# One Trainium2 core, two transformer blocks: the order and place of the small transfers at the front, column sums of the modulation, gates of the experts' rows, and two norms behind the experts

## What is computed

```python
# block 1
mod = silu(c) @ w_mod + b_mod                 # 6 x 1024 columns, for c and for c_ctx
h, hc = modulate(rmsnorm(x)), modulate(rmsnorm(ctx))
q, k, v, r = split(h @ w_in)                  # the same for hc
z = (h @ w_ga) @ w_gb + b_g                   # rank 16, two directions
logdecay = log_sigmoid(z) / 16
o = gated linear attention, forwards and backwards over the tokens
x = x + g1 * ((rmsnorm(o) * silu(r)) @ w_out)
h2 = modulate(rmsnorm(x))
scores = sigmoid(h2 @ w_router)               # 16 experts, 2 chosen per token, in one group of 4
f = sum over chosen experts of gate * ((silu(h2 @ w1) * (h2 @ w3)) @ w2)
x = rmsnorm(x + g2 * f) * final_g
# block 2: x and ctx_2 are normed and modulated with mod_w_2, then latent and grouped attention
# (ab), a second residual, window attention and a short convolution (cd), a third residual
```

## Time and profile before

| | us |
|---|---|
| median of 3 runs | 1193.26 |
| the runs | 1191.73, 1193.26, 1199.64 |
| the profiled execution, whole | 1190.98 |
| its span, first to last instruction | 1189.2 |
| PE busy | 1020.5 (86%) |
| PE weight loads busy | 551.7 (46%) |
| DVE busy | 366.7 (31%) |
| ACT busy | 297.6 (25%) |
| mean granted PE clock | 0.943 |
| HBM read | 211.26 MB |

### The profile page before, as it was taken

How to read it: one execution, slowest core, us unless ns; L and a number is a source line. 1 busy time by engine, 2 the same in 40 slices (tenths; PEclk the granted TensorE clock), 3 DMA queues, 4 the chain that set the end, 5 groups by cost and what they waited for, 6 DMA issues and landing times.

```text
span 1189.2 us, 12358 instructions
## 1 busy us (share of the span) xinstructions
PE 1020.5 (86%) x4434; PEld 551.7 (46%) x4435; DVE 366.7 (31%) x850; ACT 297.6 (25%) x674; POOL 23.0 (2%) x41
## 2 busy tenths in 40 slices
PE   0899979989977877878768899989999897897998
PEld 0454436546543322323222555557555443575773
DVE  0200273561424100000000413057676511254451
ACT  0410422322223000000000232146665501214330
POOL 2000000000000000000000100000000000000000
PEclk9899899998977989889898999989999999898999
DMA  9925031779055699998999520201645212142220
GB/s 272 365 77 208 0 142 36 280 265 372 2 202 222 235 396 396 398 350 303 397 397 394 190 71 13 87 33 35 230 161 142 72 35 71 43 146 96 71 71 36
DMA packets 102233, 217.43 MB, mean 183 GB/s; under 512 B 5909, under 2 KB 8137, under 8 KB 102057
## 3 DMA queue, kind: packets, MB, share of 16 engines
q1 hardware_dynamic: 94480, 206.45, 47.9%
q10 hardware_dynamic: 6312, 6.03, 1.6%
q0 software_dynamic: 1392, 4.31, 1.4%
HBM read 211.26 MB, written 5.51 MB: 182 GB/s over the span
## 4 chain that ended last, share of the span: by engine, by line
PE 69%; DMA 13%; DVE 7%; ACT 5%; issue 3%; ACTq 2%; POOLq 0%; SPq 0%; POOL 0%; DVEq 0%
PE bank L527 24%; DMA arena<-in_w_up_e_dram 10%; PE bank L539 8%; PE bank L725 8%; PE bank L796 4%; PE bank L495 3%; PE bank L879 3%; PE bank L898 3%; PE bank L889 3%; DMA arena<-in_mod_w_dram 2%; PE bank L482 1%; PE bank L713 1%; PE bank L738 1%; PE bank L577 1%; PE bank L791 1%
## 5 line engine op out<-in xcount | busy, mean ns | idle before, releaser
L527 PE MATMUL bank<-arena 128*128 128x512 f32 (+3 forms) x768 | 308.3, 560 | 6.6 <-ACT arena L1128 5.1
L527 PEld LDWEIGHTS bank<-arena 128*128 128x128 f32 x768 | 145.7, 192 | 159.5 <-issue 143.1
L725 PE MATMUL bank<-arena 128*64 128x512 f32 x544 | 139.8, 671 | 32.3 <-issue 29.6
L725 PEld LDWEIGHTS bank<-arena 128*64 128x64 f32 x544 | 52.4, 153 | 118.8 <-issue 113.5
L539 PE MATMUL bank<-arena 128*128 128x256 f32 (+1 forms) x384 | 99.3, 418 | 2.8 <-ACT arena L1449 1.5
L539 PEld LDWEIGHTS bank<-arena 128*128 128x128 f32 x384 | 72.7, 191 | 31.7 <-issue 22.2
L738 PE MATMUL bank<-arena 128*64 128x512 f32 x272 | 62.1, 597 | 9.6 <-ACT arena L1298 9.0
L495 PE MATMUL bank<-arena,silu_c 128*32 128x512 f32 x384 | 51.2, 657 | 19.5 <-ACT silu_c L1141 10.1
L1296 ACT ACTIVATE arena<-bank 128x256 f32<-128x256 f32 x16 | 6.1, 383 | 217.3 <-PE bank L725 217.3
L1857 DVE TENSOR_TENSOR arena<-arena,bank 128x256 f32<-128x256 f32 x16 | 6.7, 422 | 154.5 <-ACT arena L1296 154.5
L879 PE MATMUL bank<-arena 64*128 64x512 f32 (+3 forms) x160 | 49.3, 561 | 4.5 <-ACT arena L1535 2.3
(11 more groups left out here) (303 smaller groups left out, 1014.7 us busy)
## 6 DMA issues: line engine op xcount, KB each, us to landing
arena<-in_w_gate_e_dram SPq DMA_DIRECT2D x16, 2048.0 KB, 16.9
arena<-in_w_up_e_dram SPq DMA_DIRECT2D x16, 2048.0 KB, 21.9
arena<-in_w_down_e_dram SPq DMA_DIRECT2D x16, 2048.0 KB, 20.2
arena<-in_w_mod_dram SPq DMA_DIRECT2D x12, 2048.0 KB, 9.5
arena<-in_mod_w_dram SPq DMA_DIRECT2D x12, 2048.0 KB, 10.9
arena<-in_gla_w_in_dram SPq DMA_DIRECT2D x6, 2048.0 KB, 12.8
arena<-in_cd_w_in_dram SPq DMA_DIRECT2D x6, 2048.0 KB, 7.8
arena<-in_ab_w_in_dram SPq DMA_DIRECT2D x5, 2048.0 KB, 9.1
```

What stands on the lines that cost most here:

```text
L527: mm = pe.matmul(ps[:, 0:n], lhs[:, k, tile * P:(tile + 1) * P], w[:, k, c0:c0 + n], start=(k == 0), stop=(k == kd_ - 1))
L725: mm = pe.matmul(up_b[64 * j:64 * j + 64, :], h[:, k, :], w13[:, :, k, 256 * j:256 * j + 256], start=(k == 0), stop=(k == KC - 1), tile_po ...
```

## The change

- **Small transfers.** `con` is reordered and split: the first 147 columns come through ACT among the rows, the rest through POOL. `gate_a`, `gate_b`, the rest of `con`, `w_route`, the gains and `final_row` are issued by POOL, the first of them after the bank `row3`, `w_route` after `z31`.
- **First fills.** SP's order is mod0, mod1, x, ctx, mod2, mod3, k; mod0 to mod3 lie in slots 0, 1, 3, 5, and the ring goes on with k in slot 2.
- **Column sums.** `mod_cols` transposes 4 x 128 columns; DVE adds the four quadrants with a reduction and then the bias.
- **Low, z, router, gate 1.** The two directions of `low` use two column strips, those of z two row strips (partitions 0 and 32), alternating. The router's product is made with `w_route` as weights in four column strips, copied to `parts` by ACT and DVE, and summed and turned with `sum_parts`. `gate(1)` becomes one bank with the two halves on partitions 0 to 63 and 64 to 127.
- **Experts.** DVE multiplies the rows with that gate as it evicts them.
- **Behind.** The gathers have a semaphore for each tile; DVE does three operations a tile; ACT sums the squares of x and of x * final_g together, and the second scale is worked out from both; ACT does `columns_0(2)` first.

```diff
         for m in range(4):
-            load_mod(m)
+            l, c = mod_chunks[m]
+            loads.append((f"mod{m}", [(slice(0, P), slice(0, KC), cols_of(a["w_mod"][0], 512 * c, 512))],
+                          (0, 1, 3, 5)[m], KC, 512))
...
+        early_columns = cols["ones"][0]
+        con_rest_in = sem("con_rest_in")
...
-                    mm = pe.matmul(ps[:, 2 * c:2 * c + 2], mod_rows[:, m % 2, c * P:(c + 1) * P], sum_quadrants,
-                                   start=True, stop=True)
+                    mm = pe.transpose(ps[:, c * P:(c + 1) * P], mod_rows[:, m % 2, c * P:(c + 1) * P], ident)
...
+                if u == 1:
+                    ps = banks.open(pe, "gate1_1", gate_bc, 4)
+                    for h in range(2):
+                        mm = pe.matmul(ps[64 * h:64 * h + 64, :], ones[:, 0:64], gate_diag[:, 4 * h:4 * h + 4, :],
+                                       start=True, stop=True, tile_position=(0, 64 * h))
+                    banks.filled("gate1_1", mm)
+                    return
...
-            for z in range(2):
-                ps = banks.open(pe, f"low{z}", low_ready, z + 1)
-                for k in range(KC):
-                    mm = pe.matmul(ps[0:GATE_RANK, :], gate_a[:, k, z, :], hT[:, k, :],
-                                   start=(k == 0), stop=(k == KC - 1))
-                banks.filled(f"low{z}", mm)
+            pe.wait_ge(small_w_in, 16 * 2)
+            ps = banks.open(pe, "low", low_ready, 2)
+            for k in range(KC):
+                for z in range(2):
+                    mm = pe.matmul(ps[32 * z:32 * z + GATE_RANK, :], gate_a[:, k, z, :], hT[:, k, :],
+                                   start=(k == 0), stop=(k == KC - 1), tile_position=(0, 32 * z))
+            banks.filled("low", mm)
...
+            for h in range(HG):
+                for z in range(2):
+                    r = slice(32 * z, 32 * z + GATE_RANK)
+                    ps = banks.open(pe, f"z{h}{z}", z_ready, 2 * h + z + 1)
+                    mm = pe.matmul(ps[:, :], gate_b[r, h * DK:(h + 1) * DK], low[r, :], start=True, stop=True,
+                                   tile_position=(32 * z, 0))
+                    banks.filled(f"z{h}{z}", mm)
...
+            pe.wait_ge(route_in, 16)
+            ps = banks.open(pe, "parts", parts_copied, 4)
+            for k in range(KC):
+                j = k % 4
+                mm = pe.matmul(ps[32 * j:32 * j + NE, 0:T], w_route[:, k, :], h2T[:, k, :],
+                               start=(k < 4), stop=(k >= 4), tile_position=(0, 32 * j))
+            banks.filled("parts", mm)
+            pe.wait_ge(parts_copied, 4)
             ps = banks.open(pe, "logits", logit_exp, 1)
             for t in range(TT):
-                for k in range(KC):
-                    mm = pe.matmul(ps[:, t * NE:(t + 1) * NE], h2T[:, k, t * P:(t + 1) * P], w_route[:, k, :],
-                                   start=(k == 0), stop=(k == KC - 1))
+                mm = pe.matmul(ps[:, t * NE:(t + 1) * NE], parts[:, t * P:(t + 1) * P], sum_parts, start=True, stop=True)
...
-            sp.dma_start(X[:, 0:2, :], a["x"][0].rearrange("(t p) d -> p t d", p=P)).then_inc(x_in, 16)
-            sp.dma_start(X[:, 2:4, :], a["ctx"][0].rearrange("(t p) d -> p t d", p=P)).then_inc(ctx_in, 16)
...
-            for ld in loads[:N_BEFORE]:
+            for i, ld in enumerate(loads[:N_BEFORE]):
+                if i == 2:
+                    sp.dma_start(X[:, 0:2, :], a["x"][0].rearrange("(t p) d -> p t d", p=P)).then_inc(x_in, 16)
+                    sp.dma_start(X[:, 2:4, :], a["ctx"][0].rearrange("(t p) d -> p t d", p=P)).then_inc(ctx_in, 16)
...
-            act.dma_start(con[:, :], a["constants"]).then_inc(con_in, 16)
-            for n, r, half in row_list:
+            for i, (n, r, half) in enumerate(row_list):
+                if i == 4:
+                    act.dma_start(con[:, 0:early_columns], a["constants"][:, 0:early_columns]).then_inc(con_in, 16)
...
+                    act.activation(gate_rows[:, 1, 0:512], ps[:, :], ACT.Copy).then_inc(gate_bc, 2)
...
-                act.wait_ge(z_ready, 4 * z + 4)
+                act.wait_ge(z_ready, 7 + z)
...
-            act.wait_ge(x_moe, 2)
-            norm(3, y_tok[:, :, 0, :], lambda t: None)
             columns_0(2)
-            act.wait_ge(block1_done, 2)
-            norm(4, view(HIGH, 4, D), lambda t: None)
+            for t in range(TT):
+                act.wait_ge(x_moe, t + 1)
+                act.activation(y_tok[:, t, 1, :], X[:, t, :], ACT.Square, accum_out=sums[:, t:t + 1])
+                act.wait_ge(xf_ready, t + 1)
+                ins = act.activation(view(HIGH, 4, D)[:, t, :], y_tok[:, t, 0, :], ACT.Square, scale=1.0 / math.sqrt(D),
+                                     accum_out=sums[:, 2 + t:3 + t])
+            link(ins)
+            link(act.activation(sums[:, 0:2], sums[:, 0:2], ACT.Ln, bias=eps, scale=1.0 / D))
+            act.activation(rstd[:, 0:2], sums[:, 0:2], ACT.Exp, scale=-0.5)
+            link(act.activation(sums[:, 0:2], sums[:, 0:2], ACT.Exp, scale=-1.0))
+            for t in range(TT):
+                ins = act.activation(rstd[:, 2 + t:3 + t], sums[:, 2 + t:3 + t], ACT.Ln, bias=eps, scale=sums[:, t:t + 1])
+            link(ins)
+            act.activation(rstd[:, 2:4], rstd[:, 2:4], ACT.Exp, scale=-0.5).then_inc(rstd_ready, 2)
             columns_0(3)
             ab_gate(2)
             ab_gate(3)
...
-                dve.tensor_tensor(dst, ps[:, 0:8].rearrange("p (c m) -> p c m", m=2), inner(bias, 2), ALU.add)\
-                   .then_inc(modcol_ready, 1)
+                quadrants = ps[:, :].rearrange("p (c j m) -> p c m j", c=4, j=4)[:, :, 0:2, :]
+                link(dve.tensor_reduce(dst, quadrants, AX.X, ALU.add))
...
+            dve.wait_ge(con_rest_in, 16)
...
+            ps = banks.wait(dve, "parts")
+            dve.wait_ge(parts_zeroed, 1)
+            for j in (2, 3):
+                dve.tensor_copy(parts[32 * j:32 * j + NE, :], ps[32 * j:32 * j + NE, 0:T]).then_inc(parts_copied, 1)
...
-                    dve.tensor_copy(y_buf[b], dn_b[:, :]).then_inc(ye_ready, 1)
+                    dve.tensor_tensor(y_buf[b], dn_b[:, :], gate_rows[:, 1, 0:512], ALU.mult).then_inc(ye_ready, 1)
...
-            dve.wait_ge(gathered_y, 16 * 4)
-            dve.wait_ge(gate_bc, 4)
             for t in range(TT):
                 ya, yb = y_tok[:, t, 0, :], y_tok[:, t, 1, :]
-                link(dve.tensor_scalar(ya, ya, gates_ab[:, t, 0:1], None, ALU.mult))
-                link(dve.scalar_tensor_tensor(ya, yb, gates_ab[:, t, 1:2], ya, ALU.mult, ALU.add))
-                link(dve.tensor_tensor(ya, ya, gate_rows[:, 1, :], ALU.mult))
-                dve.tensor_tensor(X[:, t, :], X[:, t, :], ya, ALU.add).then_inc(x_moe, 1)
-            dve.wait_ge(rstd_ready, 4)
-            dve.wait_ge(final_in, 16)
+                dve.wait_ge(gathered_y[t], 16 * 2)
+                link(dve.scalar_tensor_tensor(X[:, t, :], ya, gates_ab[:, t, 0:1], X[:, t, :], ALU.mult, ALU.add))
+                dve.scalar_tensor_tensor(X[:, t, :], yb, gates_ab[:, t, 1:2], X[:, t, :], ALU.mult, ALU.add)\
+                   .then_inc(x_moe, 1)
+                dve.wait_ge(x_moe, t + 1)
+                if t == 0:
+                    dve.wait_ge(final_in, 16)
+                dve.tensor_tensor(ya, X[:, t, :], final_row, ALU.mult).then_inc(xf_ready, 1)
+            banks.wait(dve, f"cT{AB_ORDER[1]}")
+            dve.wait_ge(rstd_ready, 5)
+            dve.wait_ge(xf_ready, 2)
             for t in range(TT):
-                dve.scalar_tensor_tensor(X[:, t, :], X[:, t, :], rstd[:, t:t + 1], final_row, ALU.mult, ALU.mult)\
-                   .then_inc(block1_done, 1)
+                dve.tensor_scalar(view(HIGH, 4, D)[:, t, :], y_tok[:, t, 0, :], rstd[:, t:t + 1], rstd[:, 2 + t:3 + t],
+                                  ALU.mult, ALU.mult).then_inc(xn_ready, 1)
+            for t in range(TT):
+                dve.tensor_scalar(X[:, t, :], y_tok[:, t, 0, :], rstd[:, t:t + 1], None, ALU.mult).then_inc(block1_done, 1)
             dve.wait_ge(block1_done, 2)
-
-            banks.wait(dve, f"cT{AB_ORDER[1]}")
-            norm_rows(4, view(HIGH, 4, D))
             turn(3, hT, [(0, T, 3)])
...
+            banks.wait(pool, "row3")
+            for z in range(2):
+                pool.dma_start(gate_a[:, :, z, :], a["gla_w_gate_a"][0, z].rearrange("(k p) r -> p k r", p=P))\
+                   .then_inc(small_w_in, 16)
+            for z in range(2):
+                pool.dma_start(gate_b[32 * z:32 * z + GATE_RANK, :], a["gla_w_gate_b"][0, z]).then_inc(gate_b_in, 16)
+            pool.dma_start(con[:, early_columns:], a["constants"][:, early_columns:]).then_inc(con_rest_in, 16)
+            banks.wait(pool, "z31")
+            pool.dma_start(w_route[:, :, :], a["w_router"].rearrange("(k p) e -> p k e", p=P)).then_inc(route_in, 16)
...
+            banks.wait(pool, "gate1_1")
```

(7 more changed lines are left out.)

70 lines of the change are left out of this document (36 added, 34 removed).

## The result

The changed kernel takes 1150.72 us (median of 4 runs, 1149.69 to 1151.7), the kernel before in the same comparison 1193.9 (4 runs, 1191.73 to 1199.64). The ratio is 0.9631 with a 95% interval of 0.9596 to 0.9666, so 3.7% faster. Forecast were 1155 us and a range of 1148 to 1167. The span fell from 1189.2 to 1149.4 us, 39.8 less; the mean granted clock rose from 0.943 to 0.952.

A forecast was written before the change was run, and what follows sets the result against it. DMA transfers were taken to bound the start, then mostly PE's or DVE's work, with weight transfers in places. Savings of 14.5 + 6.9 + 6.6 + 2.0 + 4.7 + 3.4 = 38.1 us gave 1155 us against 1193.26, range 1148 to 1167.

The forecast's parts named there:

- The front: Start to first projection: with fewer bytes ahead, mod3 lands at 30.0 and the projection starts at 39.5, 14.5 us earlier.
- The full ring: At the start, the fourth modulation chunk waited for slot 0 until 33.55; named as meeting the DMA bound there.
- The fear that the small transfers come too late: Rival: `gate_a`, now behind `row3`, lands too late for low at 85; 1193 or more, chance 0.03.
- Low and z: Gate projection and z tiles: paired strips save 6.9 us in low and 6.6 in z.
- VectorE's pace of evictions: At z: if PE had to keep DVE's pace, z takes 5.4 us and the sum is 1.9 smaller; in first rival.
- The 3.2: In the old z of 10.09 us: about 3.2 of the 6.6 us saving was the clock.
- The v tiles' clock: v tiles behind z: 13.9 us again if the clock stays up, 2.0 saved.
- the first rival: Behind z the clock falls all the same, or PE keeps DVE's pace: 4 us less gain, 1159, chance 0.17.
- Column sums: adaLN chunk sums by transposes: 0.5 us less per chunk where PE is the chain, together 4.7 us.
- Router: Router logits: four strips, copies and summing take 3.5 us instead of 6.98, saving 3.4, between 1 and 5.
- Experts and behind them: Expert stage and the work after it: 0 gain, with 20 us of cover before PE asks for x.

The follow-up runs named there:

- two variants of the front: Changed kernel with old ring slots and SP order, 1154.67 us; changed kernel with its whole start undone, 1166.16 us.
- By the experiment: Changed kernel with the router's logits as before, 16 matmuls for two token tiles instead of four column groups: 1157.43 us, ratio 0.9707 to before.
- the experiment with the old form: Changed kernel with everything behind the router as before (gate row, evictions, final_row, gathers, DVE operations, norms): 1151.78 us, ratio 0.9661 to before.
- the twelve variants: Twelve kernels, each the changed kernel with parts put back, moved or reordered; medians from 1143.44 to 1168.37 us.

## Why the prediction was right, and where its steps were off

**The front.** Forecast 14.5, measured 15.2. Landing 30.71 for the forecast 30.0, start 38.90 for 39.5: PE's row behind the landing took 1.97 at full clock instead of 3.22, which is luck, as two variants of the front had it at 3.6. The reason given, full DMA engines and the bytes ahead of the last weights, was right for what stays: 10.6 MB at 387 GB/s. What was taken away isn't worth its bytes. The gains alone are 8.9 of the 15 and 1.7 by their bytes; the earlier trace rows had shown them as 6.3 us of engine time. The full ring, which I named beside the bound, costs nothing. The fear that the small transfers come too late didn't come true: `gate_a`, issued at 33.02 to 35.03, landed some 7.5 us behind its issue, and low starts at 84.86.

**Low and z.** 6.9 forecast and measured; z 6.6 and 6.5. VectorE's pace of evictions did not hold PE: 3.63 is below 8 evictions' time. The 3.2 that I had put down to the clock in the old z is what the experiments leave for it too. What I had not seen is that the border between strips alone is worth 1.4 to 1.7 us.

**The v tiles' clock.** Forecast 2.0, measured 0.3. This is the step that failed, by the first rival: I took the clock as kept, and it fell behind z all the same, at 109.4 us, though for 3.4 us instead of the 8 I had allowed. Of eleven traces with the new z, the changed kernel's among them, it fell there in five. So 1.7 us of this term, and more in one of the five, go one way or the other from kernel to kernel.

**Column sums.** Forecast 4.7, measured about 5.0 between the two traces: 0.4 for chunks 4 and 5, 1.9 for the others of the scan, 2.7 in the attention. Each is 0.67 for four transposes against 0.98, so 0.3 and not the 0.5 that I took, and 0.45 in the attention; that the total came out is partly luck.

**Router.** Forecast 3.4, measured 4.6. The parts took 1.06 at full clock, not 1.7 at the lower one that I had carried over from the earlier trace rows; the copies ran side by side on ScalarE and VectorE in 0.9. By the experiment about 2 of the 4.6 are the clock, which was low at this place in the kernel before and not in the changed one.

**Experts and behind them.** Forecast 0 for both, and the experiment with the old form confirms it. Between the traces there were 1.6 in the experts, more than the 1 that I had allowed, where the last up product took 8.78 before and 7.09 after and the clock was at 0.92 and 0.94 in the mean; −3.1 at the context tiles; 0.9 and some 1.7 in the stages behind. All of that is clock: it was at 0.50 from 621.4 to 628.3 after, and from 794.3 to 801.1 and 838.7 to 842.1 before. The context tiles show it plainly: the same 32 instructions took 14.00 before and 17.06 after. Busy time by stretch at their start, before and then after:

```profile
659.50:663.50 4.00, 3.92 (x9) 1.82 (x10) 0.00 (x0) 0.03 (x1) 0.93 (x2) 1.00 0.63 243
```

```profile
622.50:626.50 4.00, 4.00 (x6) 1.42 (x6) 0.00 (x0) 0.00 (x0) 1.62 (x2) 0.50 1.00 365
```

In the twelve variants the same 32 instructions took 15.4 to 17.1 us, never 14.0. Since the whole old form of that part also took 17.05, its edits aren't the cause; what is stays open.

**The sum.** The forecast of 38.1 against 39.8 in the spans comes from +0.7 at the front, −1.7 at the v tiles, +0.3 for the column sums, +1.2 in the router and about +1.1 net of clock in stages that the change doesn't touch. It is closer than its terms deserve: of the 39.8, the clock gave about 2 in the router and 1.3 at the last row of the front. The medians lie 43 apart and not 40, since the profiled execution of the kernel before, 1190.98, was 2.9 below its median.

## What to carry to other kernels

A broadcast of a small vector to 128 partitions is not small: the engine time of its queue (6.3 us) came nearer to its cost (8.9) than its bytes (1.7). Issue it behind the weights that the first product needs. When a wait is shortened, read what is next in the list of each engine on that chain: a change of VectorE's order alone gave 4.3 of 8 us (1.6 of it clock), and ScalarE's copy in front of a ready exponential held the other 3.7. Compare single traces step by step against a third one in which the step isn't touched, since the clock alone moves a step by 1.5 to 3 us.

## What the runs showed of the hardware

- Eleven broadcasts, 0.64 MB to 128 partitions, pulled the total rate down to 92 to 129 GB/s with the DMA engines busy all the time, and delayed the weights by 8.9 us; the same eleven to one partition each delayed them by 0.5.
- Products in two column strips overlap also where the strip changes just once: 12.21 against 13.91 us for 32 instructions.
- ScalarE's issue of a 64 KB transfer of short rows took 7.67 us at the start, behind two of the same size that it issued in 1.26; GpSimd issued two in 2.01 us at 33 us.
- The clock's falls differ between kernels that are the same up to that place: behind z in five traces of eleven. Where it fell with the new z it was for 3.4 us (6.8 in one), with the old one for 10.3 and 13.7.
